# Reordering a hybrid mixer stage: last attention tiles first on TensorE, transposes between them, an earlier norm root, and running sums inside a projection

## What is computed

```python
proj = h @ w_in                                   # 1024 -> 3344 columns
mq, mk, mv, mo, mi, mf, z, xbc, dt_raw, dq, dk, dv = split(proj)
y_mlstm = sigmoid(mo) * rms_norm(mlstm_chunkwise(mq, mk, mv, mi, mf))   # 4 heads of 64
xbc = silu(causal_dwconv(xbc))                    # 1024 channels, 4 taps
y = ssd_chunked(xs, dt, A, Bm, Cm) + D * xs       # needs running sums of dt * A
y_ssm = rms_norm(y * silu(z), per group of 256)   # 2 groups
a = softmax(q1 k1 + bias) - lam * softmax(q2 k2 + bias)                 # 4 heads
y_diff = rms_norm(a @ v)
out = concatenate([y_mlstm, y_ssm, y_diff]) @ w_out                     # x = x + out
```

## Time and profile before

| what | value |
|---|---|
| median of the runs shown | 3347.13 us (3346.76 to 3349.18) |
| the profiled execution | 3357.01 us |
| its span in the profile | 3354.9 us |
| TensorE busy | 3104.1 us, 93% |
| VectorE, ScalarE, GpSimd busy | 49%, 31%, 7% |
| mean granted TensorE clock | 0.954 |

### The profile page before, as it was taken

One profiled execution on the slowest core, in us unless ns is written; L12 is line 12 of the kernel. 1 busy time (PEld: TensorE's weight loads), 2 busy tenths in 40 slices (PEclk: granted clock), 3 DMA queues, 4 the chain that ended last, 5 costly groups with the idle time before them and its releaser, 6 DMA issues. The chain is left out here.

```text
span 3354.9 us, 42170 instructions
## 1 busy us (share of the span) xinstructions
PE 3104.1 (93%) x17336; PEld 2366.9 (71%) x17336; DVE 1649.9 (49%) x3141; ACT 1051.9 (31%) x2148; POOL 221.9 (7%) x167
## 2 busy tenths in 40 slices
PE   8999989969999999999989879999898999788887
PEld 6777768857888878888778758888686888333333
DVE  5444484365555555555674555444644674311212
ACT  4222244343323243333344343222332553000002
POOL 0000022121000000000021220000000110000000
PEclk9999989879999999999999879999889899899999
DMA  5544421102223222222211112232212004899997
GB/s 189 187 160 153 141 86 51 38 26 85 93 86 116 81 98 82 69 77 77 93 51 51 39 38 80 91 112 82 81 61 76 2 2 177 341 421 421 421 422 328
DMA packets 66168, 443.39 MB, mean 132 GB/s; under 512 B 7476, under 2 KB 7732, under 8 KB 19640
## 3 DMA queue, kind: packets, MB, share of 16 engines
q1 hardware_dynamic: 61632, 425.75, 33.5%
q10 hardware_dynamic: 2648, 8.39, 0.7%
q0 software_dynamic: 1696, 6.55, 0.5%
HBM read 435.16 MB, written 5.51 MB: 131 GB/s over the span
## 5 line engine op out<-in xcount | busy, mean ns | idle before, releaser
L157 PE MATMUL ps<-b,b 128*128 128x512 f32 (+6 forms) x14038 | 2805.9, 392 | 149.6 <-DVE b L167 48.6
L157 PEld LDWEIGHTS ps<-b,b 128*128 128x128 f32 (+3 forms) x14038 | 2100.8, 183 | 819.4 <-issue 308.7
L167 DVE TENSOR_TENSOR b<-b,b 128x512 fp32r<-128x512 f32 (+9 forms) x741 | 610.3, 828 | 284.0 <-ACT b L388 162.3
L388 ACT CAST b<-b 128x1024 fp32r<-128x1024 f32 (+2 forms) x408 | 391.7, 961 | 421.7 <-PE ps L157 414.5
L167 DVE TENSOR_TENSOR b<-ps,b 128x64 f32<-128x64 f32 (+5 forms) x626 | 220.1, 366 | 309.0 <-PE ps L157 250.3
L167 POOL TENSOR_TENSOR b<-b,b 128x1024 fp32r<-128x1024 f32 (+3 forms) x114 | 187.4, 1659 | 1383.2 <-ACT b L388 951.6
L157 PE MATMUL ps<-b 64*64 64x64 f32 (+10 forms) x2848 | 250.7, 277 | 28.9 <-ACT b L2009 15.8
L157 PEld LDWEIGHTS ps<-b 64*64 64x64 f32 (+3 forms) x2848 | 213.3, 160 | 61.4 <-issue 20.2
L177 DVE SCALAR_TENSOR_TENSOR b<-ps,b 128x512 f32<-128x512 f32 (+3 forms) x272 | 142.5, 546 | 211.3 <-PE ps L157 185.9
L183 ACT ACTIVATE b<-b 128x512 f32<-128x512 f32 (+7 forms) x287 | 151.2, 533 | 218.0 <-DVE b L177 177.0
L167 DVE TENSOR_TENSOR b<-b,ps 128x512 f32<-128x512 f32 (+1 forms) x114 | 77.1, 678 | 279.3 <-PE ps L157 276.5
(11 more groups left out here) (106 smaller groups left out, 567.4 us busy)
## 6 DMA issues: line engine op xcount, KB each, us to landing
b<-in_eg SPq DMA_DIRECT2D x64, 1024.0 KB, 27.4
b<-in_eu SPq DMA_DIRECT2D x64, 1024.0 KB, 27.2
b<-in_ed SPq DMA_DIRECT2D x64, 1024.0 KB, 26.8
b<-in_wg SPq DMA_DIRECT2D x44, 1024.0 KB, 4.8
b<-in_wu SPq DMA_DIRECT2D x44, 1024.0 KB, 4.9
b<-in_win SPq DMA_DIRECT2D x40, 1024.0 KB, 4.8
b<-in_wd SPq DMA_DIRECT2D x48, 768.0 KB, 4.2
b<-in_wmod SPq DMA_DIRECT2D x24, 1024.0 KB, 5.0
```

The lines of the kernel that those rows point to most:

```text
L157: return e.h.matmul(out, l, r, start=start, stop=stop)
L167: return e.h.tensor_tensor(out, a, b, op)
L388: e.h.copy(hi, src).then_inc(*self.S.tick(("hi", i)))
```

## The change

The attention steps keep their order, but the steps around them move. `ssq 1`, `sroot` and `snorm 0` move from behind tile 14 to between tiles 12 and 15. The step `turn` keeps the transposes alone, and casts and low parts become a step `parts`. Blocks 0 and 1 are transposed before 4 and 5, which go to banks 2 and 3, and `mo` comes before tile 16. `diff 18` and the transposes of all SSM blocks now stand before `part 0` and `part 1`. In the head of the stage `cum` moves between the halves of item 7 and `xs` and `bias` between the halves of item 8; each bank of `xs` waits for its own reader alone. The low part of item 3 is made by VectorE. Two storage areas are exchanged to suit.

```diff
--- before.py
+++ after.py
@@ -1571,9 +1571,9 @@
         self.hp = k.parts(k.hTf, k.low)
         places = [cut(at + 512 * i, 512) for at, n in ((4224, 11), (12576, 5)) for i in range(n)]
         self.raw = [(k.fr(places[2 * c]), k.fr(places[2 * c + 1])) for c in range(8)]
-        self.order = (2, 3, 4, 5, 0, 1, 6, 7)
+        self.order = (2, 3, 0, 1, 4, 5, 6, 7)
         self.opp = {c: (k.fr(cut(at, 512)), k.fr(cut(at + 512, 512))) for c, at in
-                    zip(self.order, (0, 1024, 4128, 5152, 3088, 7456, 8736, 12064))}
+                    zip(self.order, (0, 1024, 3088, 7456, 4128, 5152, 8736, 12064))}
         self.items = []
         win = k.A["win"][l]
         for kind, name, first, n in (("fm", "xbc", 2, 4), ("fm", "qk", 0, 2), ("tok", "V1", 8, 1), ("fm", "dqk", 6, 2),
@@ -1640,7 +1640,7 @@
 
     def lower(self, i):
 
-        return self.V if i < 3 else self.G
+        return self.V if i < 4 else self.G
 
     def there(self, i):
 
@@ -1657,7 +1657,7 @@
             self.load_sp(e, i)
         yield
 
-    CUT = {13: 2, 14: 1, 15: 1, 16: 2, 17: 2, 18: 1, 21: 2, 22: 2, 23: 2, 24: 2}
+    CUT = {6: 0, 7: 0, 13: 2, 14: 1, 15: 1, 16: 2, 17: 2, 18: 1, 21: 2, 22: 2, 23: 2, 24: 3}
 
     def behind(self, i):
 
@@ -1671,8 +1671,9 @@
             yield "ones", 0
         elif i == 5:
             yield "gates", 0
+        elif i == 6:
+            yield "cum", 0
         elif i == 7:
-            yield "cum", 0
             yield "xs", 0
             yield "bias", 0
         elif i == 8:
@@ -1701,14 +1702,20 @@
             yield "diff", 0
             yield "diff", 1
         elif 20 < i < 25:
-            for j in range(2):
-                yield "diff", 3 * (i - 21) + 3 + j
+            yield "diff", 3 * (i - 21) + 3
+            if i == 24:
+                yield "ssq", 1
+            yield "diff", 3 * (i - 21) + 4
             yield "mnorm", i - 16
+            if i == 24:
+                yield "sroot", 0
             yield "diff", 3 * (i - 21) + 5
         if i in (21, 23):
             yield "zgate", i // 2 - 10
-        elif i in (22, 24):
-            yield "ssq", i // 2 - 11
+        elif i == 22:
+            yield "ssq", 0
+        elif i == 24:
+            yield "snorm", 0
 
     def steps(self):
         yield "zero", 0
@@ -1730,34 +1737,35 @@
             n = self.CUT.get(i, len(todo))
             yield from todo[:n]
             left = todo[n:]
-        diff = 15
-        yield "sroot", 0
-        yield "snorm", 0
-        for n in range(diff, 19):
-            yield "diff", n
-            if n == 15:
-                yield "turn", 2
-                yield "turn", 3
-            elif n == 16:
-                yield "snorm", 1
-                yield "turn", 4
-                yield "turn", 5
-            elif n == 17:
-                yield "mo", 0
-                yield "dnorm", 0
-                yield "dnorm", 1
-                yield "turn", 0
-                yield "turn", 1
-                yield "part", 0
-            elif n == 18:
-                yield "part", 1
+        yield "diff", 15
+        yield "turn", 2
+        yield "turn", 3
+        yield "mo", 0
+        yield "diff", 16
+        yield "parts", 2
+        yield "parts", 3
+        yield "turn", 0
+        yield "turn", 1
+        yield "snorm", 1
+        yield "diff", 17
+        yield "dnorm", 0
+        yield "dnorm", 1
+        yield "parts", 0
+        yield "parts", 1
+        yield "turn", 4
+        yield "turn", 5
+        yield "diff", 18
         yield "dnorm", 2
         yield "dnorm", 3
-        yield "dnorm", 4
-        for t in range(4):
-            yield "dnorm", 5 + t
-        yield "turn", 6
-        yield "turn", 7
+        yield "parts", 4
+        yield "parts", 5
+        yield "part", 0
+        yield "part", 1
+        for t in range(5):
+            yield "dnorm", 4 + t
+        for c in (6, 7):
+            yield "turn", c
+            yield "parts", c
         for i in range(self.np, len(self.items)):
             yield from self.ahead(i)
             yield "sum", i
@@ -1791,7 +1799,7 @@
         return [j for j in range(i) if self.items[j].kind == "tok" and self.items[j].half == self.items[i].half][-1:]
 
     def turn_bank(self, c):
-        return {0: 0, 1: 1, 6: 2, 7: 3, 2: 4, 3: 5, 4: 4, 5: 5}[c]
+        return {0: 0, 1: 1, 6: 2, 7: 3, 2: 4, 3: 5, 4: 2, 5: 3}[c]
 
     def y_of(self, t, c):
         if c < 2:
@@ -1906,9 +1914,10 @@
             elif name == "diff":
                 self.diff_pe(e, i)
             elif name == "xs":
-                e.wait_ge(V.at("Bg"), V.at("small_tr"))
                 for j in range(4):
                     b = B[self.XB[j]]
+                    if j > 1:
+                        e.wait_ge(V.at("Bg" if j == 2 else "small_tr"))
                     for c in range(4):
                         e.wait_ge(V.at(("xbc", j)))
                         p = k.tr(e, b[:, c * 128:c * 128 + 128], self.xbc[:, j, 3 + c * 128:131 + c * 128])
@@ -1947,13 +1956,13 @@
                 p.then_inc(*P.tick(("ssd", h)))
             elif name == "turn":
                 if i in (4, 5):
-                    e.wait_ge(V.at(("snorm", 3, 1)), V.at(("ylo", i - 2)))
+                    e.wait_ge(V.at(("snorm", 3, 1)), V.at(("L", 15, i - 4)))
                 elif i in (2, 3):
                     e.wait_ge(V.at(("snorm", 3, 0)), S.at(("put", 17, 0)))
                 elif i < 2:
                     e.wait_ge(V.at(("mnorm", 3)), S.at(("put", 25, 0)))
                 else:
-                    e.wait_ge(V.at(("dnorm", 3)))
+                    e.wait_ge(V.at(("dnorm", 3)), V.at(("ylo", i - 2)))
                 for t in range(4):
                     p = k.tr(e, B[self.turn_bank(i)][:, t * 128:t * 128 + 128], self.y_of(t, i))
                 p.then_inc(*P.tick(("turn", i)))
@@ -2178,7 +2187,7 @@
             elif name == "sroot":
                 e.wait_ge(V.at("srec"))
                 act(e, self.sms, self.sms, ACT.Sqrt).then_inc(*S.tick("srs"))
-            elif name == "turn":
+            elif name == "parts":
                 e.wait_ge(P.at(("turn", {0: 1, 6: 7}.get(i, i))))
                 e.h.copy(self.op(i)[0], B[self.turn_bank(i)][:, :]).then_inc(*S.tick(("yhi", i)))
             yield
```

## The result

| | before | changed | ratio (95% interval) |
|---|---|---|---|
| median | 3348.15 us (3346.76 to 3350.62, 4 runs) | 3300.46 us (3299.8 to 3301.13, 4 runs) | 0.9855 (0.9841 to 0.9869) |
| profiled execution, span | 3357.01, 3354.9 us | 3301.13, 3299.3 us | |
| mean granted clock | 0.954 | 0.966 | |

Repeated in two later sessions, the changed kernel's medians were 3303.48 and 3302.6 us, with executions from 3298.4 to 3308.6, beside 3348.44 and 3352.03 us of before.

What follows compares the result with a forecast made beforehand. The prediction took TensorE as the bound almost everywhere, but an engine-to-engine chain at the mixer stage's end. 2 x 13.0 + 5.4 + 4.8 - 0.2 = 36.0 us off 3347.13 gave 3311 us, range 3302 to 3324.

Steps and rivals of the forecast that it cites:

- term 1: End of each mixer stage: the reordered chain through VectorE saves 13.0 us a mixer, bounds 10.5 to 15.5.
- term 2: Head of each stage: TensorE's wait for the copy of Bg shrinks, saving 5.4 and 4.8 us, bounds 3.5 to 6.5.
- `mo` plus 1.0 us: End of the stage: `mo` takes its old 1.84 us and 1.0 us more for GpSimd running beside it.
- rival 2: TensorE keeps its higher level through the stage's end: 14.9 us each end, 42.6 in all, about 3304.5 us; chance 0.13.
- The attention norm: End of the stage: the projection covers this norm, its 2.07 us wait goes and 1.7 us are left.
- The table loads: ScalarE around the moved root: two loads of 1.28 us, the second hidden in a 1.64 us wait, costed at nothing.
- Rival 1: VectorE beside GpSimd becomes the bound, so only 26 to 28 us are gained, about 3320 us; chance 0.2.
- Term 3: Item 3's low part on VectorE: net 0.1 us lost, twice, 0.2 us in all.

Runs made afterwards that it cites:

- the head alone: Kernel before with `cum` between the halves of item 7, `xs` between those of item 8, item 3's low part on VectorE: 3338.81 us, ratio 0.9962.
- the root alone: Kernel before with only group 1's squares, the root and `snorm 0` moved earlier, the order of transposes and last V product unchanged: 3336.13 us, ratio 0.9958.
- the late product: Changed kernel with the last V product and the attention norm's squares back behind the projection's first 18 matmuls: 3308.9 us, ratio 0.9883.
- the fillers: Kernel before with 30 unused transposes of a constant in each of TensorE's two long waits at a stage's end: 3347.92 us, ratio 0.9999.

## Why the prediction was wrong

The direction and the mechanism were right: the end of the stage is a chain through VectorE, it is gained twice, the head's wait is the third piece, and nothing of it is given back. What failed is **the size of term 1**, 13.0 us a mixer where the profile shows 17.3 and 17.2, above its own bound of 15.5 too. Of the 11.7 us between 36.0 and 47.7, term 1 makes 8.5 and term 2 makes 1.6.

- `snorm 0`, forecast from 726.2 to 727.9 in the old count, ran from 726.1 to 727.8 (715.92 and 717.59, plus the 10.2 us between the landmarks). The stalled maximum of tile 15, forecast to end at 732.6, ended at 732.5.
- **`mo` plus 1.0 us was counted twice.** The row of 1.84 us held a collision with GpSimd already; `mo` took 1.83 us. 1.1 us too much. With only 8 columns of GpSimd's subtraction left, so that its squares lay elsewhere, `mo` took 1.43.
- **TensorE's level was rival 2's, at 0.13.** Transposes of blocks 4 and 5: 1.09 for 1.97, 0.9 us. The 36 matmuls: 8.60 for 9.59, 1.0 us. The 60 behind the stage, in no sum of mine, nor in rival 2's: 14.42 for 15.61, 1.2 us. With 13.2 and 1.1 these make 17.4 (the rows overlap a little, and from start to start the first two are 0.7 and 0.8). I had priced the path with rows taken behind waits of 7 us, which the change removes. Only the transposes of blocks 0 and 1, behind 2.82 us, kept 1.97. The windows show the level itself (columns as in the earlier trace rows), two of before and one of the changed kernel:

```profile
731.00:754.80 23.80, 10.50 (x45) 9.41 (x46) 14.44 (x30) 9.78 (x20) 4.42 (x4) 0.50 0.12 44
768.60:771.90 3.30, 3.30 (x10) 2.52 (x9) 0.78 (x2) 0.51 (x2) 2.37 (x1) 0.50 0.00 0
724.00:727.30 3.30, 3.18 (x16) 3.18 (x17) 3.19 (x8) 1.32 (x4) 0.62 (x1) 0.50 0.66 271
```

The kernel before had the lower level from inside the first long wait to the projection's first matmuls, and again right behind the stage. The changed kernel has it from 724.0 to 727.3 us, and from 727.5 to 790 its granted clock is 1.00.

- The attention norm was off the path as forecast; its slack is 0.95 us, not 1.7, since the projection it hides behind is faster.
- The table loads cost nothing. The drain that "ScalarE: Activation LUTs" (section "What ACT_TABLE_LOAD costs" of the Trainium skill) adds is not in these rows: the square root begins 0.01 us behind its load, and the second load ended at 715.70 and delayed nothing.
- Rival 1 did not happen. VectorE was stalled only where it read SBUF twice or held small operations: the maximum's last step took 0.93 us and ended with GpSimd's subtraction (722.32 and 722.30), but the reductions beside it took 0.64 each. "SBUF — State Buffer" (section "SBUF: two separate sides", Trainium skill) says that whichever engine starts first holds the shared port pair for its whole instruction and the other is blocked. The trace agrees in that the stalled step ends with the subtraction. It was stalled by 0.76 us, not by a whole subtraction of 2.35.
- **Term 2** forecast 5.4 and 4.8 us and measured 6.1 and 5.7 by rows, 11.1 by the run of the head alone. In the first mixer the wait fell by 6.3: 1.00 where 1.5 was forecast, since the 12 matmuls of item 7 took 2.8 us and not 3.2, so its half was done 0.5 us later than I had it. The transposes saved 1.8 at the higher level, 24 matmuls behind `cum`, at 0.30 us where 0.24 is the full level, took 1.4 back, and the wait that grew from 0.38 to 0.83 took 0.4.
- **Term 3**, a loss of 0.1 us a mixer, did not come: the stretch it lies in takes 6.38 us for 6.41.
- The sum by rows: 17.3 + 17.2 + 6.1 + 5.7 = 46.3, of 47.7 measured. The rest is within the scatter of executions.

The range was too narrow, because term 1 and its bounds held the level at what the rows of before showed, and only a rival at 0.13 let it rise. How much of the level's 3 us a mixer the change earns stays partly open. For it: five of the six ends of the changed kernel read 25.11, and the next 60 matmuls take 14.4 us where only the 1.47 us wait stands ahead of them, but 15.6 where the 2.07 us wait stands there too (before, the root alone, the head alone, the late product). Against: the sixth end, and the kernel with GpSimd's subtraction cut, lost time at the same place (2.7 us in the sixth end, 3.1 and 1.7 in the two of the cut kernel, from the transposes of blocks 4 and 5 on), and the fillers won rows in one execution and no time in the median.

## What to carry to other kernels

When a reorder removes long waits from a chain, price the instructions behind them with rows taken while TensorE was busy, and the ones that keep their wait with the old rows; put the difference into the range. A duration that already holds a collision is not charged for it again. Before laying work into a wait, walk the supply of the next item (unit free, cast, low part), since a covered wait of 2.8 us came back as one of 2.64.

## What the runs showed of the hardware

- TensorE's level can differ between executions of one kernel at one place: the 36 matmuls of the first mixer took 8.60, 9.76 and 8.61 us in three profiles of the changed kernel.
- Shorter idle time does not always mean the higher level. With the subtraction cut, behind waits of 1.65, 0.61 and 1.66 us, eight transposes took 1.97 us; in the changed kernel, behind 2.82 and 1.34, they took 1.09. What decides it these runs do not settle.
- A GpSimd subtraction of 2.35 us from and to SBUF stalled a VectorE operation on 2 columns for 0.76 us and left reductions alone (0.64 us a piece). A VectorE operation that reads PSUM took its usual 0.69 us beside another such subtraction (743.56, GpSimd from 742.52 to 744.92).
